# The sums over partitions of the modulation vectors: matmuls against ones, or transposes summed by VectorE

## The reference

```
def _modulation(cvec, w, b):
    m = jax.nn.silu(cvec) @ w + b
    m = m[..., None, :]
    return m[..., :D_MODEL], m[..., D_MODEL:2 * D_MODEL], m[..., 2 * D_MODEL:]

shift, scale, gate = _modulation(c, mod_w, mod_b)
shift_c, scale_c, gate_c = _modulation(c_ctx, mod_w, mod_b)   # attention layer only
h = _rmsnorm(x, pre_g) * (1 + scale) + shift
x = x + gate * _rmsnorm(y @ w_out, post_g)
```

## Time and profile before

| | us |
|---|---|
| median of 3 runs (lowest, highest) | 2078.82 (2078.52, 2085.97) |
| span of the profiled execution, first to last instruction | 2067.7 |
| TensorE matmuls busy | 2012.8 |
| VectorE busy | 1608.2 |
| ScalarE busy | 934.2 |
| the 12 sums' matmuls | 256 passes |
| granted clock of TensorE, mean over the span | 0.986 |

### The profile page before, as it was taken

One profiled execution on the slowest core, in us unless ns is written; L12 is line 12 of the kernel. 1 busy time (PEld: TensorE's weight loads), 2 busy tenths in 40 slices (PEclk: granted clock), 3 DMA queues, 4 the chain that ended last, 5 costly groups with the idle time before them and its releaser, 6 DMA issues.

```text
span 2067.7 us, 37414 instructions
## 1 busy us (share of the span) xinstructions
PE 2012.8 (97%) x13770; PEld 1846.8 (89%) x13770; DVE 1608.2 (78%) x2164; ACT 934.2 (45%) x1334; POOL 169.9 (8%) x264
## 2 busy tenths in 40 slices
PE   7999999999999999999999998999999997999997
PEld 7998898898889998889988897887789995899996
DVE  6986676658888878888878887678887777687755
ACT  6553446555444334443334554245463344444442
POOL 0000000021000000000101111011100120001011
PEclk9999999999999999999999999999999998999998
DMA  6554453356777887777878865576647772668652
GB/s 235 165 158 136 172 189 116 103 171 211 231 233 231 265 286 239 236 235 251 271 262 297 289 215 174 177 249 213 197 162 233 265 273 98 199 212 277 194 190 92
DMA packets 119573, 434.34 MB, mean 210 GB/s; under 512 B 13217, under 2 KB 13601, under 8 KB 119217
## 3 DMA queue, kind: packets, MB, share of 16 engines
q1 hardware_dynamic: 90672, 328.11, 48.2%
q0 software_dynamic: 28800, 104.87, 15.3%
HBM read 430.83 MB, written 2.10 MB: 209 GB/s over the span
## 4 chain that ended last, share of the span: by engine, by line
PE 84%; DVE 10%; issue 2%; DMA 2%; ACT 1%; POOL 0%; SPq 0%; POOLq 0%; ACTq 0%; DVEq 0%
PE ps L586 25%; PE ps L587 13%; PE ps L573 12%; PE ps L574 12%; PE ps L575 12%; DVE w_lo L1460 3%; PE ps L674 1%; PE ps L997 1%; DMA side<-w_side 1%; PE ps L669 1%; PE ps L1007 1%; PE ps L710 1%; DVE mod_sum L1477 1%; DVE sq L1533 1%; ACT w_hi L1091 0%
## 5 line engine op out<-in xcount | busy, mean ns | idle before, releaser
L1460 DVE TENSOR_TENSOR w_lo<-raw,w_hi 128x1024 fp32r<-128x1024 f32 x610 | 734.8, 1246 | 51.1 <-ACT w_hi L1091 49.1
L1091 ACT ACTIVATE w_hi<-raw 128x1024 fp32r<-128x1024 f32 x610 | 622.0, 1054 | 317.5 <-PE ps L575 305.0
L586 PE MATMUL ps<-a_act,w_hi 128*128 128x512 f32 x2112 | 748.9, 398 | 6.9 <-DVE a_act L1543 4.3
L587 PE MATMUL ps<-a_act,w_lo 128*128 128x256 f32 x2112 | 592.6, 281 | 0.0
L586 PEld LDWEIGHTS ps<-a_act,w_hi 128*128 128x128 f32 x2112 | 397.2, 188 | 105.1 <-issue 6.7
L573 PE MATMUL ps<-b_act,w_hi 128*128 128x256 f32 x1536 | 439.2, 286 | 2.4 <-DVE b_act L1953 1.7
L574 PE MATMUL ps<-b_act,w_hi 128*128 128x256 f32 x1536 | 436.6, 284 | 0.0
L575 PE MATMUL ps<-b_act,w_lo 128*128 128x256 f32 x1536 | 436.5, 284 | 0.0
L587 PEld LDWEIGHTS ps<-a_act,w_lo 128*128 128x128 f32 x2112 | 400.2, 189 | 0.7 <-issue 0.7
L573 PEld LDWEIGHTS ps<-b_act,w_hi 128*128 128x128 f32 x1536 | 296.8, 193 | 3.0 <-DVE b_act L1953 1.9
L574 PEld LDWEIGHTS ps<-b_act,w_hi 128*128 128x128 f32 x1536 | 296.8, 193 | 0.0
(11 more groups left out here) (320 smaller groups left out, 1816.2 us busy)
## 6 DMA issues: line engine op xcount, KB each, us to landing
raw<-w_main SPq DMA_DIRECT2D x610, 512.0 KB, 4.4
side<-w_side POOLq DMA_DIRECT2D x200, 512.0 KB, 4.6
x_tok<-x_in SPq DMA_DIRECT2D x4, 512.0 KB, 7.2
ctx_tok<-ctx_tok SPq DMA_DIRECT2D x1, 2048.0 KB, 11.4
y_out<-o_tok SPq DMA_DIRECT2D x4, 512.0 KB, 3.0
table<-counts_tab SPq DMA_DIRECT2D x1, 512.0 KB, 13.1
cons<-cons_in SPq DMA_DIRECT2D x1, 478.0 KB, 10.6
table<-masks_in SPq DMA_DIRECT2D x1, 448.0 KB, 10.5
```

What stands on the lines that cost most here:

```text
L586: pe.matmul(ps[:, bank, :], wh, act[:, kt, :, :], start=first and b == 0, stop=False)
L587: mm = pe.matmul(ps[:, bank, 0:T], wl, act[:, kt, 0, :], start=False, stop=last and b == 7)
L1091: act.activation(w_hi[:, slot, :], raw[:, slot, :], ACT.Copy).then_inc(hi_ready, 1)
L1460: dve.tensor_tensor(w_lo[:, slot, :], raw[:, slot, :], w_hi[:, slot, :].bitcast(F32), ALU.subtract)\
```

## The change

`sum_mods` takes one vector at a time. For the nine groups whose stage has no entry in `MOD_BANK`, each of the vector's eight blocks is transposed into two PSUM banks (6 and 7 for a group of one vector; 4 and 5 for the first, 6 and 7 for the second of a group of two), and VectorE sums the two banks along the free axis before it adds the bias. The groups of `ev_kv`, `ev_q` and `ev_q2` keep the matmuls against ones and the single small read. The second vector of a pair is transposed one step after the first and read one step after it. `mods_summed` counts vectors (`mod_sums`). VectorE writes out three steps instead of two at the start of 16-step stages with a group.

```diff
+def mod_vecs(stage):
+    return 2 if MOD_GROUPS[stage] in BOTH else 1
+def mod_sums(stage, c):
+    return sum(mod_vecs(n) for n in MOD_STAGES[:MOD_STAGES.index(stage)]) + c + 1
...
-                    if stage in SUMS_OF and isinstance(i, int) and k == SUMS_STEP.get(stage, 0):
-                        sum_mods(SUMS_OF[stage])
+                    if stage in SUMS_OF and isinstance(i, int):
+                        c = k - SUMS_STEP.get(stage, 0)
+                        if 0 <= c < mod_vecs(SUMS_OF[stage]):
+                            sum_mods(SUMS_OF[stage], c)
...
-                summed = mods_of(stage)
-                vecs = len(summed)
+                summed = mods_of(stage)[c]
                 for t in range(8):
-                    for c in range(vecs):
-                        mm = pe.matmul(ps[:, MOD_BANK.get(stage, 7), vecs * t + c:vecs * t + c + 1], summed[c][:, t * P:(t + 1) * P],
-                                       ones[:, 0:1], start=True, stop=True)
+                    block = summed[:, t * P:(t + 1) * P]
+                    if stage in MOD_BANK:
+                        mm = pe.matmul(ps[:, MOD_BANK[stage], t:t + 1], block, ones[:, 0:1], start=True, stop=True)
+                    else:
+                        mm = turn(block, (6 if mod_vecs(stage) == 1 else 4 + 2 * c) + t // 4, (t % 4) * P)
                 mm.then_inc(mods_summed, 1)
...
-            def read_mods(stage):
...
-                dve.tensor_tensor(mods[:, t0:t0 + 8, 0:vecs],
-                                  ps[:, MOD_BANK.get(stage, 7), 0:8 * vecs].rearrange("p (m c) -> p m c", c=vecs),
-                                  vbc(col("mod_b", t0, 8), vecs), ALU.add).then_inc(S("mods_read"), 1)
+            def read_mods(stage, c=0):
+                t0, vecs = 8 * MOD_GROUPS[stage], mod_vecs(stage)
+                dst = mods[:, t0:t0 + 8, c]
+                dve.wait_ge(mods_summed, mod_sums(stage, c))
+                if stage in MOD_BANK:
+                    summed = ps[:, MOD_BANK[stage], 0:8]
+                else:
+                    bank = 6 if vecs == 1 else 4 + 2 * c
+                    turned = ps[:, bank:bank + 2, :].rearrange("p a (m n) -> p (a m) n", n=P)
+                    then(dve.tensor_reduce(dst, turned, AX.X, ALU.add))
+                    summed = dst
+                ins = dve.tensor_tensor(dst, summed, col("mod_b", t0, 8), ALU.add)
+                if c == vecs - 1:
+                    ins.then_inc(S("mods_read"), 1)
...
-                    if stage in SUMS_OF and isinstance(i, int) and k == SUMS_STEP.get(stage, 0) + 1:
-                        read_mods(SUMS_OF[stage])
+                    if stage in SUMS_OF and isinstance(i, int):
+                        c = k - SUMS_STEP.get(stage, 0) - 1
+                        if 0 <= c < mod_vecs(SUMS_OF[stage]):
+                            read_mods(SUMS_OF[stage], c)
...
-                    first = COUNT[stage] if COUNT[stage] != DT else max(first, 2)
+                    first = COUNT[stage] if COUNT[stage] != DT else max(first, 3)
```

More of the change, by code:

```diff
@@ L105, in low_outs @@
     return sum(COUNT[n] for n in JOINT[:JOINT.index(stage)]) + k + 1
+BOTH = (0, 1, 2, 3)
 MOD_BANK = {"ev_kv": 4, "ev_q": 6, "ev_q2": 6}
+def mod_vecs(stage):
+    return 2 if MOD_GROUPS[stage] in BOTH else 1
+def mod_sums(stage, c):
+    return sum(mod_vecs(n) for n in MOD_STAGES[:MOD_STAGES.index(stage)]) + c + 1
 SUMS_OF = {"down0": "up0", "up1": "down0", "down1": "up1", "up2": "down1", "up2b": "up2", "down2": "up2b",
@@ L111 @@
 SUMS_STEP = {"ev_q2": 1, "ev_z": 1}
-BOTH = (0, 1, 2, 3)
 CMP_AT = 0
@@ L655, in body, with turn, sum_mods @@
                     if stage in SUMS_OF and k == SUMS_STEP.get(stage, 0):
-                        sum_mods(SUMS_OF[stage])
+                        sum_mods(SUMS_OF[stage], 0)
                 steps(pe, stage, body, first=COUNT[stage] if chain is not None else 2 if reads is not None else 0)
-            def sum_mods(stage):
+            def turn(src_ap, bank, at_col, rows=P, ncols=P, base=0):
+                return pe.transpose(ps[0:ncols, bank, at_col:at_col + rows], src_ap, ident[base:base + rows, base:base + rows])
+            def sum_mods(stage, c):
                 g = MOD_STAGES.index(stage)
@@ L664, in sum_mods @@
                     pe.wait_ge(S("e_rot"), 6 if stage == "ev_q" else 10)
-                summed = mods_of(stage)
-                vecs = len(summed)
+                summed = mods_of(stage)[c]
                 for t in range(8):
-                    for c in range(vecs):
-                        mm = pe.matmul(ps[:, MOD_BANK.get(stage, 7), vecs * t + c:vecs * t + c + 1], summed[c][:, t * P:(t + 1) * P],
-                                       ones[:, 0:1], start=True, stop=True)
+                    block = summed[:, t * P:(t + 1) * P]
[3 more added lines that the diff above has]
+                        mm = turn(block, (6 if mod_vecs(stage) == 1 else 4 + 2 * c) + t // 4, (t % 4) * P)
                 mm.then_inc(mods_summed, 1)
-            def turn(src_ap, bank, at_col, rows=P, ncols=P, base=0):
-                return pe.transpose(ps[0:ncols, bank, at_col:at_col + rows], src_ap, ident[base:base + rows, base:base + rows])
             def norm(name, bank=2):
@@ L1030, in _ @@
             norm("od")
-            sum_mods("ev_out")
+            sum_mods("ev_out", 0)
             run("od_u", a_act, split=[("norm_lo", normed("od", -1))])
@@ L1047, in _ @@
                 if g == 0:
-                    sum_mods("od_z")
+                    sum_mods("od_z", 0)
             pe.wait_ge(silu_ready, FFN_TILES + 33)
@@ L1479, in add_mod @@
                 ins.then_inc(mods_added, 1)
-            def read_mods(stage):
-                g, t0 = MOD_STAGES.index(stage), 8 * MOD_GROUPS[stage]
-                vecs = 2 if MOD_GROUPS[stage] in BOTH else 1
-                dve.wait_ge(mods_summed, g + 1)
-                dve.tensor_tensor(mods[:, t0:t0 + 8, 0:vecs],
-                                  ps[:, MOD_BANK.get(stage, 7), 0:8 * vecs].rearrange("p (m c) -> p m c", c=vecs),
-                                  vbc(col("mod_b", t0, 8), vecs), ALU.add).then_inc(S("mods_read"), 1)
+            def read_mods(stage, c=0):
[12 more added lines that the diff above has]
+                    ins.then_inc(S("mods_read"), 1)
             def reading(stage, read, first=0, chain=None, after=None):
```

## The result

| | before | after |
|---|---|---|
| median, us (n; lowest, highest) | 2078.67 (6; 2071.71, 2085.97) | 2055.80 (6; 2052.67, 2062.22) |
| span of the profiled execution | 2067.7 | 2053.3 |
| its device time | not given | 2055.22 |
| mean granted clock | 0.986 | 0.988 |

The ratio is 0.9903, with an interval of 0.988 to 0.9925. So the kernel is faster, by 15.6 to 24.9 us. Most of what follows is about those 11 us.

The account below looks back on a forecast made before the run. TensorE, busy 97% of the span, was taken as the bound. Its 16.8 us gain, less 0.1, 1.4, 0.9 and 0.6, made 13.8; less 1.7, 12.1, so a median of 2066.7 us, range 2061 to 2073.

Parts of the forecast that it names:

- launch and end: Outside the profiled span: the 11.1 us between the span of 2067.7 and the median of 2078.82, left unchanged.
- The price of a vector, 0.88 against 1.79 us: TensorE, at each sum: eight transposes cost 0.88 us, one-column matmuls 1.79, so a vector saves 0.91.
- The rival that took a transpose's record for its price: At the bursts: eight transposes cost 8 x 0.28 = 2.2 us against 1.79, giving 2086; chance 0.04.
- The tiles being fresh: At the bursts: full-clock bursts in the trace read tiles written long before, counted for the rival with chance 0.04.
- The four falls of clock, 1.47 each: Half clock behind sums in `down0`, `down1`, `up2`, `down2`: all four go, 1.47 us each, 5.9 in all.
- The reason given, a burst half as long as what drew none: Clock behind bursts: 0.88 us of transposes, half of the 1.79 us sums that drew no fall, should draw none.
- The beat of `up1`, 1.7 charged: TensorE's rhythm in `up1`: might go from good to bad, 0 to 3.4 us lost; the middle, 1.7, taken.
- VectorE in `up2` and `up2b`, 1.4 lost: VectorE nearly the bound there: of TensorE's 4.19 us gain 2.8 remain, 1.4 lost; `up2b` gains nothing.
- `od_u`, 0.9 lost: Start of `od_u`: the reduction pushes `w_lo` back 1.28 us, less 0.33 it waited for ScalarE; 0.9 lost.
- `od_out`, 0.6 lost: Before `od_out`: the reduction ahead of `w_lo` makes it ready at 1959.2 against 1958.6; 0.6 us lost.
- `down2`, 2.3 gained: In `down2`: TensorE gains 0.91 + 1.47 = 2.38 us, of which 0.1 is lost to VectorE.

Follow-up runs that it names:

- both vectors at once: Changed kernel with the transposes of both vectors of a pair behind the first step: 2059.3 us, ratio 0.9922 to the kernel before.
- long bursts: Changed kernel with both vectors of a pair behind the first step and every transpose done twice: 2067.12 us, ratio 0.9961 to the kernel before.
- the `ev_out` group by ones: Changed kernel with the `ev_out` group kept as matmuls against ones in bank 7: 2055.31 us, ratio 0.9904 to the kernel before.
- only the split: Changed kernel with every sum as matmuls against ones, a pair's second vector still one step later: 2067.64 us, ratio 0.9958 to the kernel before.

## Why the prediction was off, step by step

**The step that failed** is in the sum: "the runs' median 2078.82 lies 11.1 above it (launch and end), which I leave alone". Launch and end are 1.9 us: 2055.22 less 2053.3 after the change, and 1.9 again in the executions of the kernel before that have both numbers (2076.22 and 2074.3; 2079.81 and 2077.9). So the first profiled execution took about 2069.6, near the fastest of the kernel before (2065.5 to 2086), and the other 9.2 us were no constant but the distance of its other executions from this one. The prediction took the falls and the beat of one profile for those of all. The error adds up: 9.2 from this step, 2.3 from the profiled span (2055.6 forecast, 2053.3 found), less 0.6 by which the median after lies above its own profiled execution: 10.9, which is 2066.7 less 2055.8. The 2.3 is 2.2 in `up2` and `up2b`, 1.7 for the beat and some small terms, less 1.4 in `od_u` and 1.1 at the start.

What the 9.2 is made of is known in part. About 3 is luck: 2078.82 is the median of three, and all 58 timed executions of the kernel before have a mean of 2075.9, 6.3 above 2069.6. Where those 6.3 lie, the profiles show: the other three of the kernel before are on average 5.9 us longer than the first, 3.0 of it in the region (longer falls, a fall in `up1`, the slow beat there), which the change takes away, and 2.9 outside it, 1.6 of which is the slow beat in `od_u`. The rest outside was not traced.

The four profiles of before have a mean span of 2072.1 and the two of after 2054.8. Of these 17.3 us the region gives 18.0 (607.9 against 589.9), and outside it 0.7 is lost. The forecast had 11.8 for the region, 13.5 before the charge for the beat. What it missed, as an estimate: the charge of 1.7; falls worth 5.25 and not 4 times 3.4 us, 1.8 more; the slow beat of `up1` in two of four, 1.6. That makes 16.9 of the 18.0. The 17.3 agrees with the second set's medians (18.7), and with the means of all executions, 2075.9 and 2057.0 (12 of the changed kernel): 18.9. The 22.9 of the first six and six is the upper part of the same interval, and some of it luck. The spread fell too: executions of the kernel before have a standard deviation of 4.1 to 6.0 us, and those of the changed kernel 2.1 and 3.2.

**The price of a vector, 0.88 against 1.79 us**: right. `up1` lost 1.82 for two, the first 15 steps of `ev_out` 0.91, the pool step 0.91; doubling the transposes added 1.76 a pair. The rival that took a transpose's record for its price fell at once, since starts stand 0.109 apart. The tiles being fresh made no difference.

**The four falls of clock, 1.47 each**: right for the profiled execution (`down0` -3.35 and `down1` -3.34 against -3.28), and too few for the typical one. The reason given, a burst half as long as what drew none, did not need to hold: bursts of 16 transposes, twice as long, drew none, and neither did bursts of 32.

**The beat of `up1`, 1.7 charged**: wrong sign. The seven profiles with transposes all have 5.55 there; of the four before, two have 5.65, so here too the change gave and did not take. Why a one-column sum leaves the slow beat and a transpose the fast one is open.

**VectorE in `up2` and `up2b`, 1.4 lost**: too large for the profiled pair. The stages got 4.98 shorter, where TensorE was to save 4.19, and `up2b`, which was to gain nothing, gained 1.95 of it. On the means it is closer to the forecast. The two stages together are 141.7 to 143.7 in four profiles of before (mean 143.0) and 138.7, 139.8 in two of after, 3.7 us less, all of it in `up2` (3.6); `up2b` is 69.7 on both sides. With the 1.25 falls that `up2` has on average, TensorE was to save 4.6, so some 0.9 was lost and not 1.4. Leaving out all reductions gave 0.1 there against the first profile after and 1.3 against the second. What the reductions cost in these two stages is below the scatter and stays open.

**`od_u`, 0.9 lost**: the wait itself is right (1.95 forecast as about 2.0, so 0.83 more). What was missed is behind it: in all four profiles that have the 1.95 us wait there (the two of the change, both vectors at once, long bursts), a fall of 3.4 us stands at its end, and the second step takes 7.05 to 7.22 us where it takes 5.6 or 5.7 otherwise, 1.4 more; in the eight with the 1.1 us wait, four of the kernel before and four of experiments, none does. The 2.26 is 0.83 + 1.43. Against the kernel before as it mostly is, the loss is smaller: three of its four profiles had the slow beat in `od_u`, 97.6 us, and none of the four profiles with the long wait has it (98.3 to 98.4).

**`od_out`, 0.6 lost**: the wait is right, 0.60. The stage lost 0.43 against the first profile of before, which had been 0.4 slower there than the other three; against those (113.6) it lost 0.83.

**`down2`, 2.3 gained**: -2.72 in the profiled pair, which had a fall there. The fall stood in two of the four profiles of before; on the means the stage gained 1.8.

## What to carry to other kernels

A profiled execution is one draw. Before a median is set against its span, find out what launch and end cost, by a run that gives both; if the rest is some microseconds, it is variation, part of it with a place in the kernel, and a change that takes away its cause gains more than the one profile shows. Here 3.5 us of one-column matmuls cost twice, in their passes and in the half clock behind them, and transposes with a reduction on an engine that had room were the cheaper form. Keep such a reduction away from the start of a stage where TensorE already waits for VectorE: in `od_u` 1.2 us of it became 2.3.

## What the runs showed of the hardware

- 32 transposes in a row, 3.5 us, were followed by full clock behind all four pairs of one profile, where 3.5 us of one-column matmuls were followed by 3.4 or 6.8 us at 1.2 GHz in 12 of 12 cases in `down0`, `down1` and `up2`, and in 2 of 4 in `up1`.
- The falls behind sums were 3.4 or 6.8 us long, and cost about 1.5 us of time for each 3.4; which of the two it is differs between executions of the same kernel.
- A fall can come with no sum right before it: at the end of the wait of 1.95 us in `od_u` in 4 of 4 profiles (1.1 us: 0 of 8), and at the end of one of 2.15 us in `down2` (the `ev_out` group by ones).
- The alternating matmuls of 512 and 256 columns have two beats, 5.55 and 5.65 us for 32. In `up1` and `od_u` the one that the third step has holds to the end of the stage; in `up2` it can change in between (5.65, then 5.55, in the second profile of before). The slow one came without a fall too (only the split, `up1`), so a fall is not what it takes. What sets it stays open; it is worth up to 3.1 us in `up1` and 1.6 in `od_u`.
